# A transformer layer on one core: the Fourier projection on split operands, its folds behind each chunk, and the modulation weights read in 32 pieces

## The reference

```python
mod_x = split(silu(c) @ w_ada + b_ada, 6)      # shift, scale, gate, and the same three for the second half
mod_c = split(silu(c_ctx) @ w_ada + b_ada, 6)  # of these only shift and scale are used
proj  = modulate(layer_norm(stream), shift, scale) @ w_in      # for latents and for context
qk_pre, v, o_pre, g, f_in = split(proj)                        # f_in: 512 columns
qk    = silu(conv3x3(qk_pre) + conv_b)                         # then a chunkwise mLSTM scan in both directions
mix   = concat([readout(mlstm(q, k, v, g), o_pre), fourier_mix(f_in)]) @ w_out
x     = layer_norm(ALPHA * x + mod_x[2] * mix) * ln1_g + ln1_b
x     = channel_residual(x, mod_x[3], mod_x[4], mod_x[5], ...)  # 64 experts, 8 for each token
```

## Time and profile before

| what | value |
|---|---|
| median of 3 runs | 1734.49 us |
| profiled execution | 1736.35 us |
| its span | 1734.5 us |
| granted TensorE clock, mean | 0.993 |
| PE busy | 1664.0 us (96%) |
| DVE busy | 1168.7 us (67%) |
| ACT busy | 837.7 us (48%) |
| POOL busy | 524.6 us (30%) |

### The profile page before, as it was taken

The page is one execution under the profiler, slowest core; times in us unless marked ns, Lnnn a source line. Parts: engine busy times, 40 slices in busy tenths (PEclk is TensorE's granted clock), DMA queues, the critical chain, the costliest instruction groups (busy, mean ns, idle before and its releaser), DMA issues.

```text
span 1734.5 us, 33491 instructions
## 1 busy us (share of the span) xinstructions
PE 1664.0 (96%) x7891; PEld 1301.1 (75%) x7892; DVE 1168.7 (67%) x1712; ACT 837.7 (48%) x1155; POOL 524.6 (30%) x557
## 2 busy tenths in 40 slices
PE   7999999988899998999999999999999999999997
PEld 1547878878644677888888777888888887888874
DVE  4786895437768788574467887572866787266647
ACT  0322334322321134565467787563866686366624
POOL 2000000025313301343334444443444444343442
PEclk9999999999999999999999999999999999999999
DMA  9740111143443424787778999685989889588764
GB/s 379 270 166 13 37 49 37 57 139 118 163 152 109 176 73 161 249 309 239 232 211 294 357 344 347 218 253 132 313 267 332 235 310 363 96 292 234 222 198 193
DMA packets 98963, 361.65 MB, mean 209 GB/s; under 512 B 19901, under 2 KB 20062, under 8 KB 90469
## 3 DMA queue, kind: packets, MB, share of 16 engines
q1 hardware_dynamic: 68754, 292.29, 44.5%
q0 software_dynamic: 30160, 68.76, 17.7%
q10 hardware_dynamic: 4, 0.02, 0.0%
HBM read 332.66 MB, written 72.72 MB: 234 GB/s over the span
## 4 chain that ended last, share of the span: by engine, by line
PE 72%; DMA 12%; DVE 8%; issue 3%; ACT 3%; SPq 1%; DVEq 1%; ACTq 0%; POOL 0%; POOLq 0%
PE psum L1438 8%; PE psum L1439 8%; PE psum L1440 8%; PE psum L1270 6%; DMA sum_rows<-arena,idxs 6%; DMA raw_weights<-in_w_gu 4%; PE psum L1462 4%; PE psum L1460 4%; PE psum L1461 4%; PE psum L1425 4%; PE psum L1118 3%; PE psum L1201 3%; PE psum L1202 3%; PE psum L1203 3%; DVE arena L1693 2%
## 5 line engine op out<-in xcount | busy, mean ns | idle before, releaser
L2092 DVE TENSOR_TENSOR split_weights<-raw_weights,split_weights (+1 forms) x366 | 428.7, 1221 | 47.4 <-ACT split_weights L738 36.0
L738 ACT ACTIVATE split_weights<-raw_weights (+1 forms) x366 | 364.1, 1059 | 40.8 <-issue 24.0
L738 ACT ACTIVATE arena<-psum 128x1024 f32<-128x1024 f32 (+4 forms) x197 | 157.6, 810 | 416.5 <-PE psum L1304 83.1
L1438 PE MATMUL psum<-split_weights,split_rows 128*128 (+1 forms) x832 | 334.4, 402 | 4.7 <-DVE split_rows L2081 2.3
L1439 PE MATMUL psum<-split_weights,split_rows 128*128 (+1 forms) x832 | 326.0, 392 | 0.0
L1440 PE MATMUL psum<-split_weights,split_rows 128*128 (+1 forms) x832 | 326.0, 392 | 0.0
L694 POOL DMA_INDIRECT sum_rows<-arena,idxs x102 | 177.8, 1743 | 233.0 <-DMA sum_rows<-arena,idxs 189.5
L1438 PEld LDWEIGHTS psum<-split_weights,split_rows 128*128 128x128 f32 x832 | 157.4, 189 | 38.5 <-issue 5.6
L680 POOL COPY idxg<-idxT 128x1 uint32 (+1 forms) x107 | 75.4, 705 | 351.1 <-DVE split_rows L2081 279.2
L1440 PEld LDWEIGHTS psum<-split_weights,split_rows 128*128 128x128 f32 x832 | 156.5, 188 | 33.1
L1439 PEld LDWEIGHTS psum<-split_weights,split_rows 128*128 128x128 f32 x832 | 156.8, 189 | 30.4
(11 more groups left out here) (319 smaller groups left out, 2558.2 us busy)
## 6 DMA issues: line engine op xcount, KB each, us to landing
raw_weights<-in_w_gu SPq DMA_DIRECT2D x62, 2048.0 KB
raw_weights<-in_w_dn SPq DMA_DIRECT2D x62, 1024.0 KB
arena<-in_w_ada SPq DMA_DIRECT2D x12, 2048.0 KB, 8.6
arena<-in_toks SPq DMA_DIRECT2D x18, 512.0 KB, 8.9
extra<-in_w_proj SPq DMA_DIRECT2D x17, 512.0 KB, 3.3
arena<-job_rows SPq DMA_DIRECT2D x16, 512.0 KB, 3.8
arena<-in_w_out SPq DMA_DIRECT2D x2, 2048.0 KB, 10.0
t_rows<-arena SPq DMA_DIRECT2D x8, 512.0 KB, 2.6
```

The costliest lines, as they stand in the source:

```text
L738: return act.activation(o, i, ACT.Copy)
L1438: mm(bank(3 + p), xk, part(par, 0, 512 * k), start=(k == 0), stop=False)
L2092: tt(cols(wsplit, (1 - par) * (2 * WE) + (WE + 1024 * c), 1024), cols(raw, (1 - par) * WE + 1024 * c, 1024), high, ALU.subtract).then_inc( ...
```

## The change

Three things change, and with them the place of many buffers.

1. The Fourier projection works on split operands, as the projection stream does. Its matmuls read `u_high`, `u_low` and split `w_f`: 4 chunks x 8 k x 2 halves x 3. The splits of `uT` and `w_f` are made ahead of or within it. The latent tiles come first (groups 2 to 5 and 6 to 9), and the two context tiles are transposed between chunk 1 and chunk 2.
2. DVE's fold of a chunk stands directly behind that chunk's copies, ahead of the next split or pieces.
3. Rows 2 to 5 of the modulation come in 32 pieces of 512 KB, eight for a row, in two buffers. POOL starts the transfers, each when the piece two before it is used; the pieces of row 0 are weighed between the folds, those of row 1 between the combinations of the transform, and those of rows 2 and 3 in four groups of four in the value and output-gate chunks. PE sums row 0 within the transform, row 1 behind the first key chunk, row 2 in the first output-gate chunk and row 3 behind the second. Buffers of the last two rows lie where the Fourier half of `mixT` was, so SP stores that half to DRAM (2 MB) and brings it back after the stream. Rows are stored by POOL instead of ACT.

The diff, cut to its core:

```diff
-        piece = [at(D0, 4096)..., at(D0 + 4096, 4096)...]
+        piece = [[at(D0 + o + 1024 * i, 1024) for i in range(2)] for o in (6144, 4096)]
-        mrows = [arena[0:1, C0 + 9216 + 1024 * i:C0 + 10240 + 1024 * i] for i in range(3)] + [arena[0:1, B0 + 8192:B0 + 9216]]
+        mrows = [arena[0:1, o:o + 1024] for o in (B0 + 8192, C0 + 13312, D0 + 7168, D0 + 7168)]
-        SUM_BEHIND = (2, 4, 5, 7)
+        ROW_BEHIND = {(0, 2): 1, (13, 0): 2, (14, 1): 3}
-        GROUPS = [(0, 2), (2, 4), (6, 4)]
+        GROUPS = [(2, 4), (6, 4), (0, 2)]
...
# POOL
+            def load_piece(i):
+                g, k = i // 8, i % 8
+                if i >= 2:
+                    pool.wait_ge(S("piece_used"), i - 1)
+                pool.dma_start(piece[g // 2][i % 2], drows(a["w_ada"], ...)[:, k, :]).then_inc(S(f"piece_in{i % 2}"), 16)
+            def load_row(g):
+                if g:
+                    pool.wait_ge(S("mrow_out"), 16 * g)
+                pool.dma_start(mrows[g], a["b_ada"][...]).then_inc(S("brow_in"), 16)
+            def store_row(g):
+                pool.wait_ge(S("mrow_ready"), g + 1)
+                pool.dma_start(grow[g:g + 1, :], mrows[g]).then_inc(S("mrow_out"), 16)
...
+            pool.wait_ge(S("fourier_rows"), 16)
+            load_row(2)
+            for i in range(16, 24):
+                load_piece(i)
+            store_row(2)
+            load_row(3)
+            for i in range(24, 32):
+                load_piece(i)
+            store_row(3)
...
# PE
+            def modulation_sum(g):
+                pe.wait_ge(S("piece_used"), 8 * g + 8)
+                if g >= 1:
+                    pe.wait_ge(S("mrow_ready"), g)
+                for h in range(2):
+                    ins = mm(bank(ROWBANKS[g][h])[0:1, :], ones[:, 0:1], wsum[g // 2][...], start=True, stop=True)
+                ins.then_inc(S("ada_mm"), 1)
...
+            token_transposes(0)
+            token_transposes(1)
+            fourier_chunk(0)
+            fourier_chunk(1)
+            token_transposes(2)
+            fourier_chunk(2)
+            fourier_chunk(3)
...
+                if (i, part) in ROW_BEHIND:
+                    modulation_sum(ROW_BEHIND[i, part])
-                if (kind, h, part) == ("out", 1, 1):
+                if (kind, h, part) == ("out", 2, 1):
                     row_columns()
...
# DVE
+            def weigh(pieces):
+                for i in pieces:
+                    g, k = i // 8, i % 8
+                    dve.wait_ge(S(f"piece_in{i % 2}"), 16 * (i // 2 + 1))
+                    if k:
+                        dve.wait_ge(S("piece_used"), i)
+                        stt(acc, src, c, acc, ALU.mult, ALU.add).then_inc(S("piece_used"), 1)
...
             fold(0)
+            fourier_low(3)
+            weigh(range(2, 4))
             fold(1)
+            weigh(range(4, 6))
             fold(2)
+            weigh(range(6, 8))
             fold(3)
...
             gate_out(0)
+            modulation_row(2)
             weight_low(NCH - 3)
+            weigh(range(24, 28))
             gate_out(1)
+            weigh(range(28, 32))
             gate_out(2)
             weight_low(NCH - 2)
             gate_out(3)
+            modulation_row(3)
+            gate_out(4)
+            weight_low(NCH - 1)
+            gate_out(5)
```

More of the change, by code:

```diff
@@ L370, in build @@
         NVAL = len(VALUES)
-        HIGH_X, HIGH_C, HIGH_W = 0, 9, 10
+        SPLITS = ["f0"] + [f"x{k}" for k in range(8)] + ["f1", "f2", "f3", "c0", "c1"] + [f"w{i}" for i in range(NCH)]
+        TOKENS = [NTC + t for t in range(NTX)] + list(range(NTC))
         PART_TILES = ((NTC, 4), (NTC + 4, 4), (0, NTC))
@@ L487, in _ @@
                 load_job(x)
-            for n_ in range(5, 8):
+            for n_ in range(6, 8):
                 store_gates(n_)
@@ L743, in _ @@
             act.wait_ge(S("front_dve"), MOD_READY_0 + 1)
-            for g, (t0, nt) in enumerate(GROUPS):
-                for k in range(0, 8, 2 if g else 1):
-                    q = 8 * g + k
-                    w = 0 if g else 1
-                    act.wait_ge(S("tr_done"), q + 1)
-                    act.activation(uT[:, k, P * t0:P * (t0 + nt)], bank(q % 4)[:, 0:P * nt], ACT.Identity,
-                                   scale=modc[:, 16 + 2 * k + w:17 + 2 * k + w], bias=modc[:, 2 * k + w:2 * k + w + 1]).then_inc(S("uT_act"), 1)
@@ L765, in _, with token_columns @@
-            act.wait_ge(S("front_dve"), MROW_READY_0 + 4)
-            act.dma_start(grow[3:4, :], mrows[3]).then_inc(S("mrow_out"), 16)
-            for c in range(4):
-                act.wait_ge(S("front_mm"), AB_DONE_0 + 2 * c + 1)
-                copy(G[0][:, c], bank(2 * (c % 2)).rearrange("p (s n) -> p s n", s=4)).then_inc(S("ab_act"), 1)
+            def token_columns(g, k):
+                t0, nt = GROUPS[g]
+                w = 1 if g == 2 else 0
+                q = 8 * g + k
+                act.wait_ge(S("tr_done"), q + 1)
+                act.activation(uT[:, k, P * t0:P * (t0 + nt)], bank(q % 4)[:, 0:P * nt], ACT.Identity,
+                               scale=modc[:, 16 + 2 * k + w:17 + 2 * k + w], bias=modc[:, 2 * k + w:2 * k + w + 1]).then_inc(S("uT_act"), 1)
@@ new lines, in modulation_sum @@
+            def modulation_sum(g):
+                pe.wait_ge(S("piece_used"), 8 * g + 8)
+                if g >= 1:
+                    pe.wait_ge(S("mrow_ready"), g)
+                for h in range(2):
+                    ins = mm(bank(ROWBANKS[g][h])[0:1, :], ones[:, 0:1], wsum[g // 2][:, 512 * h:512 * h + 512], start=True, stop=True)
+                ins.then_inc(S("ada_mm"), 1)
+            pe.wait_ge(S("const_in"), 16)
+            token_transposes(0)
+            token_transposes(1)
@@ L1721, in _ @@
             weight_low(NCONV + 3)
+            weigh(range(16, 20))
             dve.wait_ge(S("rl_step"), 3)
```

349 lines of the change are left out of this document (193 added, 156 removed).

## The result

The changed kernel takes 1751.81 us (median of 4 runs, 1750.84 to 1753.1); the kernel before took 1734.72 in the same comparison (4 runs, 1734.25 to 1736.59). The ratio is 1.0089, with a 95% interval from 1.0073 to 1.0104: slower by 0.9%, 17.1 us. The profiled executions, 1751.19 against 1736.35, differ by 14.8 us.

The account below looks back on a forecast made before the run. PE was taken to bound the kernel (72% of the chain of waits). Terms -10.7 + 1.8 + 1.4 + 1.8 + 10.8 + 2.0 sum to +7.1 us: 1741.6 us; range 1733 to 1750.

Parts of the forecast that it names:

- front, at the stream's start: Before the projection stream: split Fourier projection and earlier folds start the stream at 139.1 instead of 149.8, -10.7 us.
- sum of row 1: PE's sum of this modulation row behind key chunk 0 of the stream, where PE sets the pace: +1.8 us.
- sum of row 2: PE's sum in the first output-gate chunk: +1.8 us, less 0.4 that PE waits anyway, so +1.4.
- sum of row 3: PE's sum of the last modulation row behind the second output-gate chunk: +1.8 us.
- wait for the eight pieces: Behind the second output-gate chunk PE waits until DVE has weighed row 3's last piece, at 358.9: +10.8 us.
- half clock behind the wait: PE's clock falls in the gap behind the second output-gate chunk: +2.0 us, 0 at best.
- L: Time from POOL's start of a 512 KB piece transfer to its landing, taken as 3.5 us.
- rival 3: POOL's transfers of pieces are slow, say 5 us each: wait 16.8, sum +14.6, 1749.1 us; chance 0.15.
- The 6.9 of the gather: Wait for a POOL gather of similar size among the experts' weights, 6.9 us; as transfer time, a wait of about 25.
- Rival 1: Row 3's pieces arrive in time, PE's wait vanishes: -5.7, 1728.8 us; milder form -2.1, 1732.4; chance 0.13 in either form.
- rival 2: Gains and losses cancel, with transfers near 3 us and half the front's losses absent: +2.4, 1736.9 us; chance 0.21.
- Rival 4: The front gives only -6 instead of -10.7, DVE late in folds and clock dropping twice: 1746.3 us; chance 0.09.

## Why the prediction was wrong

The direction, the places and the mechanism were right; the time came out at 1751.8 where I said 1741.6, beyond the end of my range at 1750. In the pair of traces 7.7 us of that miss can be followed; the rest is that the two profiled executions lie closer together than the medians. By its terms:

| term | predicted | measured |
|---|---|---|
| front, at the stream's start | -10.7 | -12.3, and 2.2 given back behind it |
| sum of row 1 | +1.8 | +1.8 |
| sum of row 2 | +1.4 | +1.3 |
| sum of row 3 | +1.8 | +1.8 of 3.5 |
| wait for the eight pieces | +10.8 | +17.3 |
| half clock behind the wait | +2.0 | +1.6, in the sum itself |
| rest | 0 | +0.2 to the stream's end, -0.7 from there to the router, +1.6 behind it |
| sum | +7.1 | +14.8 |

- **The failed step is the size of L, the transfer in each turn.** I wrote L = 3.5 from SP's row of 3.3, because the DMA engines "have a share of only 0.35 here". The four transfers on the chain took 4.7 in the mean, and 0.28 of issue stands ahead of three of them: 4 x 1.2 and 0.8 make 5.6. The same mistake in small: the store of row 2, for which I took 2.3, landed 3.4 us after its start, and 5.3 us passed from the row to the first load instead of 3.0. That four products and not five stand on the chain takes 1.3 back: 5.6 + 2.3 - 1.3 = 6.6, and the wait was 6.5 us longer. My rival 3, with L = 5, gave +14.6 and came nearest. That it agrees so closely with 14.8 is partly luck: it had 1.2 too much for the transfers and 1.5 for a loss in the front that did not come, and nothing for the longer store. Two of its neighbours were also added up loosely: by the prediction's own terms L = 2.6 gives a wait of 7.2 (it says 6.9, and uses 6.6), and L = 6.9 a sum of +22 instead of +24. Nothing hangs on either.
- **Why 3.5 was wrong.** The row of 3.3 is mostly of loads that SP starts one at a time. The last transfer on the chain, 3.86, shows what a piece takes with hardly another in flight: it started at 352.04, the piece before it landed at about 352.3, and from 352 to 356 us the DMA engines moved 131 GB/s, which is this one piece. The same holds for the last piece of row 1, started at 130.82 and landed 3.9 us later. So about 0.4 of the 1.2 us is there even for a lone piece, and the rest, 5.0 in the mean of the other three, came where pieces overlapped. Of pairs started 1.4 us apart the second was the slow one: at 116.44 and 117.84 us they took 3.9 and 5.0. SP's own load in the stretch of the gates took 4.3. Under such load SP's queue was no faster (4.05 to 5.31). The 0.4 of the lone piece may lie partly in the place of the rows: with rows that lie together the last transfer took 3.54. Size is shown (2.3 at a quarter). That transfers in flight lengthen one another fits all of this, and also the kernel with four buffers and the later sum, where more of them overlap (its issues between 322 and 352 us):

```profile
arena<-in_w_ada POOLq DMA_DIRECT2D x7, 512.0 KB, 7.3
```

  It was not tried by itself: no kernel here runs the whole loop with one piece in flight, so that the overlap is the cause is read from the traces and not shown by an experiment.
- **The 6.9 of the gather** was too far on the other side: that transfer ran with the DMA engines full. The mean of the two rows, 5.1, would have been nearer than either.
- **The front** came out 1.6 us better at the stream's start and 2.1 worse behind it, so the net was right (8.9 forecast with the first sum, 8.4 measured), with some luck: a clock loss of 2 us was in both, but not in the same place. Chunk 0 at 58.55 against 57.9, the gap at the context tiles near 4 us (80.8 to 84.7, against 4.3), and DVE late for the stream, all as said. But the cause of the lag was half missed: I counted DVE's work and not the turns of row 1's pieces, which are on the chain from 116 us on. I had put the half clock into chunk 0; in this execution it fell at the stream's start.
- **The clock behind the hole** cost 1.6 us instead of 2.0, since the sum of 1.8 us took nearly all of the slow stretch.
- **Rivals.** Rival 1 needed L under 1.4, rival 2 near 3: both out. Rival 4 (the clock falling twice in the front) was not what happened in the profiled execution, but it does occur (below).

The Trainium skill (DMA: Bandwidth & Descriptors, "Anatomy of one DMA — SWDGE (gpsimd) path") led to an estimated 3.2 us. The trace does not agree: the measured median of 4.3 is a third above it, and even the 3.86 of the nearly lone piece is a fifth above it. For 128 KB the same page gives an estimated 2.3 (2.0 and 0.3), and 2.3 was measured. So the rule held for the small transfers; for the large ones it is too short, alone and more so two at a time.

## What to carry to other kernels

When a change puts a chain of load, use, load into an engine's list, its price is turns times (start + transfer + use), and the transfer's time must be read where as many transfers are in flight as there will be; here the row of lone transfers was the lowest value (3.3, against 3.9 for a nearly lone piece and 5.0 with pieces overlapping). What a small store or load costs when it stands in front of the chain in the same queue has to be counted too: here it was a third of the hole. The cures are cheap once the chain is seen: start the first loads ahead of anything that waits, move the consumer one step later, or give the chain one more buffer, and ask of each wait whether the clock falls behind it.

## What the runs showed of the hardware

- The clock behind one and the same wait is not the same in each execution. All kernels here but the one before share the front up to chunk 0. In 13 profiled executions of it chunk 0 began at full clock in seven, and in six with a mean of 0.50 to 0.63 over its first 3 us. The kernel with four buffers and the later sum had such a loss three times, at 58, at 85 and at 139 us; the first and the last:

```profile
58.00:61.00 3.00, 3.00 (x9) 2.35 (x8) 3.00 (x4) 2.71 (x5) 1.36 (x2) 0.50 0.49 101
...
139.00:142.00 3.00, 1.75 (x4) 1.49 (x5) 2.43 (x5) 0.00 (x0) 0.00 (x0) 0.65 0.01 1
```

  It spanned 1737.3 us, while its runs went from 1727.8 to 1739.3. At the stream's start, behind a wait of 2.4 to 3.2 us, the clock was down in all eleven executions with that wait (means of 0.50 to 0.75 from 139 to 142 us), and in neither of the two without it (waits of 0.68 and none).
- A normalisation of a token tile (DVE, 0.81 us) took 3.10 us where a memset of the general engine ran (75.39 to 77.5 us). That the memset is the reason was not tried. Of the kernel after:

```profile
74.47 0.81 DVE L1640 TENSOR_SCALAR arena<-arena,mv,rstd 128x1024 f32<-128x1024 f32 x1
75.20 3.10 DVE L1640 TENSOR_SCALAR extra<-extra,mv,rstd 128x1024 f32<-128x1024 f32 x1
```

  It cost nothing here, since DVE was ahead.
- A store of one row of 4 KB by the general engine took 3.4 us from start to landing at the gates, more than a load of 128 KB (2.3). The median of the four such stores in the kernel after is 1.6.
